# Moving a block of multiply-and-sums from the gate stretch into the attention stretch of a one-core hybrid layer

## The chip, the cores and the metric

The kernel runs on one core of a Trainium2 chip. The metric is device time in microseconds (us) of one execution. TensorE is called PE below (PEld is its weight load), VectorE DVE, ScalarE ACT, GpSimd POOL, and SP is the engine that issues most DMAs.

## What is computed

One layer for 128 context tokens and 512 latent tokens of width 1024. What matters here, cut from the reference:

```
mod = (silu(cond) @ w_ada + b_ada).reshape(N_MOD, D_MODEL)
shift1, scale1, gate1, shift2, scale2, gate2 = mod
h = rmsnorm(x, g_pre_mix) * (1 + scale1) + shift1
(na_q, na_k, na_v, m_q, m_k, m_v, m_o, m_i, m_f, cv_b, cv_c, cv_x, gate_pre) = split(h @ w_in)
s = concat(q @ k_neighbours + bias + column_mask, q @ k_ctx)      # 512 latent tokens, 8 heads x 64
p = softmax(s);  att = p_loc @ v_neighbours + p_ctx @ v_ctx
...                                                               # mLSTM branch hm, convolution branch hc
g = sigmoid(gate_pre + b_gate)
merged = g0 * (att @ w_br_na) + g1 * (hm @ w_br_m) + g2 * (hc @ w_br_cv)
x = x + gate1 * rmsnorm(merged @ w_out, g_post_mix)
h2 = rmsnorm(x, g_pre_ffn) * (1 + scale2) + shift2
x = x + gate2 * rmsnorm((silu(h2 @ w_ffn_gate) * (h2 @ w_ffn_up)) @ w_ffn_down, g_post_ffn)
```

The "late modulation" is the part of `mod` that nothing needs before the output projection: gate1, scale2 and shift2 (the code numbers them 2, 4 and 3). Each is 1024 columns, so eight blocks of 128 columns. There are 24 such blocks, each for two condition vectors (latent and context).

## The kernel before, in words

**Precision.** Large products are done in three passes on PE: each operand is split into a high part (`w_hi`, `h_hi`, rounded) and a rest (`w_lo`, `h_lo`), and `three` (lines 2106 to 2108) multiplies hi by hi, hi by lo and lo by hi. ACT makes the high part of a weight block (`split_hi`, line 1117), DVE the rest (`split_low`, line 1495).

**Weights.** All weights are stored as blocks of 128 x 1024 numbers (512 KB). SP loads them in one fixed order into a ring of four slots, `raw`. Block b goes to slot b % 4, and its load (line 854) waits until block b - 4 has been used up: for a weight, until its rest has been made (`lo_done`); for a block of the late modulation, until its sums are done (`ada_done`). `w_hi` and `w_lo` have four slots each too, and a slot is written again when PE has finished with the block in it.

**The plan.** `make_plan` writes out one list of steps, and every engine walks through the same list and takes from it what is its own, in order. So the place of a step in the list sets the order on each engine, and semaphores do the rest. `split` is the step that splits a weight block (or works on a block of the late modulation), `group` a product on PE with the drain of its PSUM bank.

**The stages around the change**, by time in the profile: the v projection ends at 57 us. Then come the projections q0, k0 (57 to 86 us), q1, k1, mq, mk and mv (86 to 242 us), each of groups of 24 matmuls of 320 columns. From 90 us on the attention is done beside them, in 18 units: 16 units of two heads and 16 query columns ("lat") and two of context ("ctx"). A unit's scores are made on PE in step `("na", 0, s)`, DVE adds bias and mask into `sx` (line 1822) and takes the row maximum (line 1825), ACT takes the exponential and the row sum (line 1365), DVE divides (lines 1838, 1841), PE transposes one unit later (line 2365), ACT copies (line 1375), and PE multiplies by the values two units later (line 2326). DVE then copies the result to `att` (line 1804).

**Bias and values.** Before the first unit two things must be there. POOL builds `bm`, bias plus mask, from `braw` in `bias(hp)` with six additions (line 1011); the first `braw` is loaded by SP (line 841). And the values must stand in another layout: POOL writes them to `vline` in DRAM with four DMAs (line 1036), and when all four have landed gathers them into `vtok` with eight DMAs of 256 KB (line 1042). On POOL these stand in this order: additions of `bias(0)`, load of the next `braw`, four writes, eight gathers. The first product with the values on PE waits for all eight.

**The late modulation before.** `ada_block` does a block: two `scalar_tensor_tensor` instructions on DVE (line 1508) multiply the 128 x 1024 block with a condition vector that stands in every partition (`condr`) and sum each row, one for each of the two vectors. The 24 blocks stand in the order of blocks between the gate and branch weights (467 to 611 us), with `ADA_PER_GATE` saying how many behind which. `condr` is loaded and passed through SiLU at 453 to 467 us. Two such blocks of the first modulation (`dot`, line 1763) are done in the same way at 39 to 50 us, with a copy of the condition vectors in `condr0`, whose place `naq` (the q of the attention) takes over afterwards.

Of the kernel before, what the change touches and what calls it, by code (L numbers as in the profile page):

```python
# [62 lines left out]
ADA_AHEAD, ADA_PER_GATE = 2, {2: (0, 0, 0, 0), 0: (1, 4, 4, 4), 1: (4, 4, 1, 0)}  # L63


def weight_units():
# [17 lines left out]
    late = [("ada", (m, j), KD, P) for m in (2, 4, 3) for j in range(KD)]  # L84
    for b in (2, 0, 1):
        if b == 0:
            u += [("mo", 0, KD, UW), ("mo", 1, KD, UW)] + [late.pop(0) for _ in range(ADA_AHEAD)]
        for i in range(4):
            u.append(("gate", (b, i), KD, UW))
            u.append(("br", (b, i), 4, UW))  # L90
            u += [late.pop(0) for _ in range(ADA_PER_GATE[b][i])]
# [6 lines left out]
    return u  # L98
# [21 lines left out]
BLOCKS = [(n, p) for n in range(len(UNITS)) for p in range(parts_of(n))]  # L120
# [13 lines left out]
UNIT_OF = {(k, w): n for n, (k, w, _, _) in enumerate(UNITS)}  # L134
NA_UNITS = ([("lat", hp, j) for hp in (0, 1) for j in range(NQB)] + [("ctx", 0, 0)]
# [35 lines left out]
def make_plan():  # L171
# [29 lines left out]
    def split_to(end):  # L201
        while ahead[0] < min(end, len(BLOCKS)):
            b = ahead[0]
            ahead[0] += 1
            plan.append(("split", b))
            if is_ada(b) and UNITS[BLOCKS[b][0]][1][1] == KD - 1:
                plan.append(("ada_fin", UNITS[BLOCKS[b][0]][1][0]))

    held = []
    side = []  # L210

    def unit(n):
        kind, which = UNITS[n][:2]
        for j, emit in enumerate(tiles(n)):
            later = 0
            if kind == "gate" and which[0] != 2:
                g0 = BLOCK_OF[n, 0]
                adas = ADA_PER_GATE[which[0]][which[1]]
                split_to(g0 + 3 + [adas // 2, (3 * adas + 3) // 4, adas, adas + (which != (1, 3))][j])
                if j % 2 == 0:  # L220
                    plan.append(("use", g0 + j // 2))
            elif kind == "br" and which[0] != 2 and which != (1, 3) and j == 0:
                split_to(BLOCK_OF[n, 0] + 3 + ADA_PER_GATE[which[0]][which[1]])
                plan.append(("use", BLOCK_OF[n, 0]))
            elif UNITS[n][:2] == ("br", (1, 3)):
# [27 lines left out]
            if side and j == 1 and UNITS[n][0] in ("q", "k", "mq", "mk"):  # L253
                plan.append(("half", len(groups)))
                plan.extend(side.pop(0))
# [62 lines left out]
    split_to(7)  # L318
    for t in range(TT):
        group("v", FIRST_ADA, t, bank=t if t < 4 else 7)  # L320
# [6 lines left out]
    while UNITS[n][0] != "out":  # L327
        kind, which = UNITS[n][0], UNITS[n][1]
        if kind != "ada":
            if kind == "mif":  # L330
# [4 lines left out]
                plan.append(("na_end",))  # L335
            elif kind == "mv":
                for t in range(TT):
                    for j in range(4):
                        if t == 0:
                            split_to(BLOCK_OF[n, 3] + 1)  # L340
                            plan.append(("use", BLOCK_OF[n, j]))
                        if side and (j % 2 == 0 or t == TT - 1):
                            plan.extend(side.pop(0))
# [178 lines left out]

def holder(b):

    b -= BLOCKS_HELD
    while b >= 0 and is_ada(b):
        b -= BLOCKS_HELD
    return b
# [49 lines left out]
def program(nc, a, out, vline, gline, xline):  # L578

    ctx = ExitStack()  # L580
    with ctx:
# [11 lines left out]
        def chain(start, *items):  # L593

            got = []
            for name, shape, dt in items:
# [65 lines left out]
        prod = [at("prod0", [P, D], MG - 2 * 1056 - 2048),  # L662
                at("prod1", [P, D], MG - 2 * 1056 - 3 * 2048 - 128 - 640 - 2560)]
# [21 lines left out]
        def sems(names):  # L685
# [16 lines left out]
        condr_in, condr_rd, ada_done, gcol_rd, gl_tr, gl_row, gl_out, g1_in, g2_in = sems(  # L702
            "condr_in condr_rd ada_done gcol_rd gl_tr gl_row gl_out g1_in g2_in")
# [17 lines left out]
        na_sc, na_add, na_max, na_exp, na_prob, na_tr, na_pt, na_pv, na_out = sems(  # L721
            "na_sc na_add na_max na_exp na_prob na_tr na_pt na_pv na_out")
# [90 lines left out]
        def held(buf, b):  # L813
# [3 lines left out]
            return buf[:, b % BLOCKS_HELD, :]  # L817
# [27 lines left out]
        def _(sp):  # L845
# [37 lines left out]
            for step in PLAN:  # L883
                if step[0] == "split":
# [3 lines left out]
                    elif step[1] + BLOCKS_HELD < len(BLOCKS):  # L888
                        load(step[1] + BLOCKS_HELD)
# [1656 lines left out]
```

## Time and profile before

| what | value |
|---|---|
| runs | 1143.97 us median of 3 (1143.1 to 1144.38) |
| profiled execution, first to last instruction | 1140.5 us, of its own time the part that the profile spans |
| PE busy | 1123.8 us (99%) |
| DVE busy | 725.8 us (64%) |
| ACT busy | 478.3 us (42%) |
| POOL busy | 70.8 us (6%) |
| chain that ended last | PE 93%, DVE 4% |
| granted PE clock | 0.998 over the span |

The median of the runs is 3.5 us above the span of the profiled execution; that is what lies before its first and behind its last instruction. The kernel uses one core, so there is no second die to compare with. PE's ends are modelled in the profile, so its busy time also counts overlaps: what tells of lost time is the start of one matmul against the start of the next.

### The profile page before, as it was taken

What the parts mean: (1) busy time and instruction counts of PE and PEld (TensorE: products, weight loads), DVE (VectorE), ACT (ScalarE), POOL (GpSimd) and SP (SyncE); (2) the same over time, 40 slices, a digit from 0 to 9 for tenths busy, and PEclk for the clock granted to TensorE, in tenths of its full rate; (3) what the DMA queues carried; (4) which work ended last, traced back from release to release, by engine and by line L of the source; (5) the groups of instructions that cost most, each with busy time, mean ns of one, the idle gap of its engine ahead of it and who ended that gap; (6) DMA issues with size and microseconds to landing.
All of it is one profiled execution on the core that took longest, in us unless ns stands there. A gap on an engine that the chain in (4) does not pass through costs nothing.

```text
span 1140.5 us, 18499 instructions
## 1 busy us (share of the span) xinstructions
PE 1123.8 (99%) x7324; PEld 1057.9 (93%) x7324; DVE 725.8 (64%) x1297; ACT 478.3 (42%) x881; POOL 70.8 (6%) x123
## 2 busy tenths in 40 slices
PE   6999999999999999999999999999999999999997
PEld 5799999889999999999999988999999999988886
DVE  5724444459575665687894546899897777633444
ACT  5624444344333344322222337645555455533431
POOL 2051111000000000400000002000000000000002
PEclk9999999999999999999999999999999999999999
DMA  9665221132522112346654235143332232315112
GB/s 374 241 208 120 74 75 38 38 111 80 70 58 72 57 57 73 128 125 189 192 184 128 74 130 165 58 162 122 124 111 75 75 140 83 111 64 195 56 37 93
DMA packets 40151, 130.22 MB, mean 114 GB/s; under 512 B 8737, under 2 KB 10305, under 8 KB 38529
## 3 DMA queue, kind: packets, MB, share of 16 engines
q1 hardware_dynamic: 36592, 121.41, 33.0%
q0 software_dynamic: 3472, 7.62, 2.4%
q8 instruction: 59, 0.97, 0.4%
q14 instruction: 28, 0.22, 0.1%
HBM read 121.64 MB, written 7.36 MB: 113 GB/s over the span
## 4 chain that ended last, share of the span: by engine, by line
PE 93%; DVE 4%; ACT 1%; issue 1%; DMA 0%; POOL 0%; POOLq 0%; SPq 0%; ACTq 0%; DVEq 0%
PE ps L2106 28%; PE ps L2108 28%; PE ps L2107 28%; PE ps L2326 1%; PE ps L2365 1%; PE ps L2349 1%; PE ps L2412 1%; PE ps L2414 1%; PE ps L2293 1%; PE ps L2416 1%; PE ps L2153 0%; PE ps L2400 0%; DMA xt<-in_x_sample 0%; DVE w_lo L1495 0%; PE ps L2398 0%
## 5 line engine op out<-in xcount | busy, mean ns | idle before, releaser
L2108 PE MATMUL ps<-h_hi,w_lo 128*128 128x320 f32 x1184 | 365.8, 309 | 0.0
L2106 PE MATMUL ps<-h_hi,w_hi 128*128 128x320 f32 x1024 | 322.5, 315 | 0.2 <-DVE w_hi L1620 0.2
L2107 PE MATMUL ps<-h_lo,w_hi 128*128 128x320 f32 x1024 | 316.3, 309 | 0.0
L2108 PEld LDWEIGHTS ps<-h_hi,w_lo 128*128 128x128 f32 x1184 | 222.3, 188 | 0.0
L1495 DVE TENSOR_TENSOR w_lo<-raw,w_hi 128x1024 fp32r<-128x1024 f32 x109 | 132.8, 1228 | 107.8 <-ACT w_hi L1117 107.3
L2106 PEld LDWEIGHTS ps<-h_hi,w_hi 128*128 128x128 f32 x1024 | 192.4, 188 | 2.4 <-DVE w_hi L1620 0.5
L2107 PEld LDWEIGHTS ps<-h_lo,w_hi 128*128 128x128 f32 x1024 | 192.5, 188 | 0.1
L2106 PE MATMUL ps<-w_hi,h_hi 128*128 128x512 f32 x378 | 149.3, 395 | 0.0
L2108 PE MATMUL ps<-w_hi,h_lo 128*128 128x512 f32 x378 | 147.3, 390 | 0.0
L2107 PE MATMUL ps<-w_lo,h_hi 128*128 128x512 f32 x378 | 147.1, 389 | 0.0
L1117 ACT ACTIVATE w_hi<-raw 128x1024 fp32r<-128x1024 f32 x109 | 113.2, 1052 | 32.8 <-PE ps L2108 32.2
L2106 PEld LDWEIGHTS ps<-w_hi,h_hi 128*128 128x128 f32 x378 | 71.0, 188 | 16.3 <-issue 1.6
L2108 PEld LDWEIGHTS ps<-w_hi,h_lo 128*128 128x128 f32 x378 | 70.9, 188 | 15.1
L2107 PEld LDWEIGHTS ps<-w_lo,h_hi 128*128 128x128 f32 x378 | 71.0, 188 | 14.1
L1208 ACT ACTIVATE gt<-ps,half_bg 128x320 f32<-128x320 f32 x48 | 25.4, 528 | 137.5 <-PE ps L2108 137.5
L2106 PE MATMUL ps<-h_hi,w_lo 128*128 128x320 f32 x240 | 74.4, 310 | 0.8 <-ACT snap L1255 0.8
L2106 PE MATMUL ps<-tt_hi,w_hi 128*128 128x320 f32 x240 | 74.2, 309 | 0.0
L2107 PE MATMUL ps<-tt_lo,w_hi 128*128 128x320 f32 x240 | 74.2, 309 | 0.0
L2108 PE MATMUL ps<-tt_hi,w_hi 128*128 128x320 f32 x240 | 74.2, 309 | 0.0
L2107 PE MATMUL ps<-h_lo,w_lo 128*128 128x320 f32 x240 | 74.2, 309 | 0.0
L1541 DVE TENSOR_TENSOR h_lo<-ff,h_hi 128x1280 fp32r<-128x1280 f32 (+1 forms) x22 | 30.5, 1428 | 64.4 <-ACT h_hi L1145 64.4
L1508 DVE SCALAR_TENSOR_TENSOR prod<-raw,condr 128x1024 f32<-128x1024 f32 x48 | 57.0, 1225 | 14.5 <-ACT condr L1329 12.9
(284 smaller groups left out, 1826.9 us busy)
## 6 DMA issues: line engine op xcount, KB each, us to landing
raw<-in_w_blocks SPq DMA_DIRECT2D x182, 512.0 KB, 3.8
ada<-in_w_first SPq DMA_DIRECT2D x8, 1024.0 KB, 19.9
xline<-x SPq DMA_DIRECT2D x5, 512.0 KB, 5.2
x<-xline SPq DMA_DIRECT2D x5, 512.0 KB, 8.0
xt<-in_x_sample SPq DMA_DIRECT2D x4, 512.0 KB, 5.1
condr<-in_cond_rows POOLq DMA_DIRECT2D x2, 1024.0 KB, 7.9
vtok<-vline POOLq DMA_DIRECT2D x8, 256.0 KB, 10.7
g<-gline SPq DMA_DIRECT2D x2, 1024.0 KB, 6.7
```

What stands on the lines that cost most here:

```text
L1117: ins = nc.scalar.activation(held(w_hi, b), raw[:, s, :], ACT.Copy)
L1208: nc.scalar.activation(gt[:, f, half(h)], bank, ACT.Tanh, scale=0.5, bias=half_bg[:, t:t + 1]).then_inc(act_drain, 1)
L1495: nc.vector.tensor_tensor(held(w_lo, b), raw[:, s, :], held(w_hi, b).bitcast(F32), ALU.subtract).then_inc(lo_done, 1)
L1508: ins = nc.vector.scalar_tensor_tensor(prod[c][:, :], raw[:, b % BLOCKS_HELD, :], 1.0, condr[:, c, :], ALU.mult, ALU.mult, accum_out=to)
L1541: nc.vector.tensor_tensor(h_lo[:, o2 + k:o2 + k + n, :], ff[:, k0 + k:k0 + k + n, :], h_hi[:, o2 + k:o2 + k + n, :].bitcast(F32), ALU.subt ...
L2106: nc.tensor.matmul(dst, wh, xh, start=first, stop=False, skip_group_check=resumed)
L2107: nc.tensor.matmul(dst, wh, xl, start=False, stop=False, skip_group_check=resumed)
L2108: return nc.tensor.matmul(dst, wl, xh, start=False, stop=last, skip_group_check=resumed)
L2293: ins = nc.tensor.transpose(turned_x(t, hh)[:, kk, :], xt[:, t, tok(4 * hh + kk)], ident)
L2326: ins = nc.tensor.matmul(dst[:, NKEY:512], src, pt[:, n % 2, i, c * P:(c + 1) * P], start=(c == 0), stop=(c == 2))
L2349: nc.tensor.matmul(A[i][:, 0:256], q, kk, start=True, stop=True)
L2365: ins = nc.tensor.transpose(A[2 + i][:, c * P:(c + 1) * P], sx[:, n % 2, i, c * P:(c + 1) * P], ident)
```

## The change

Three things are changed.

1. The 24 blocks of the late modulation move in the order of blocks (`EARLY_RING`) from the gates to between the blocks of k0 to mv, and on DVE to 58 to 210 us in the times of before: eight blocks before the first attention unit, then one to each of the first 15 units, and one more in mk0. A block is done in halves (`ada_half`): the product with the first vector right behind the row maximum of a unit, the second behind its division. The second half writes its products over the block itself. The weights' own splits keep their order, but stand one to two steps later or earlier. `w_hi` and `w_lo` slots are now counted by weights alone (`w_slot`).
2. The condition vectors are now `conda`, a copy of `condr0` by one SBUF to SBUF DMA of 1 MB on SP. It is issued between the load of block 10 and the load of the first `braw`. ACT's first write of `naq` waits for it, and so does the first half. `condr` is still loaded at 453 us, for a later use (line 1683).
3. Bias addition and row maximum, one addition of 768 and one reduction of 768 for a unit, become two `tensor_tensor_reduce` of 384, one for a head, that add, change the sign, and give the minimum. ACT's exponential takes the sign back by its scale. PE and POOL wait for `na_max` where they waited for `na_add`.

The order of PE's instructions is the same before and after, line by line.

```
+LATE_ADAS = [(m, j) for m in (2, 4, 3) for j in range(8)]
+EARLY_RING = ("v.0 v.1 v.2 v.3 q0.0 q0.1 k0.0 + k0.1 + + q1.0 + + q1.1 + + k1.0 "
+              "+ + k1.1 + mq0.0 + mq0.1 + mq1.0 + + mq1.1 + mk0.0 + mk0.1 + mk1.0 + + + mk1.1 + mv.0 "
+              "+ mv.1 + mv.2 +").split()
...
     split_to(7)
+    plan.append(("conda",))
...
+                elif step[0] == "ada_rest":
+                    load(step[1] + BLOCKS_HELD)
+                elif step[0] == "conda":
+                    sp.wait_ge(condr0_rd, 1)
+                    sp.wait_ge(dot_done, 2 * len(DOT_CHUNKS))
+                    sp.wait_ge(gemm_done, gid("ada_row", ("first", DOT_CHUNKS[0] - 1)) + 1)
+                    sp.dma_start(conda[:, :, :], condr0[:, :, :]).then_inc(conda_in, 16)
...
                     act.wait_ge(gemm_done, g + 1)
+                    if (which, f, h) == (0, 0, 0):
+                        act.wait_ge(conda_in, 16)
...
+            def ada_half(b, c):
...
+                s = b % BLOCKS_HELD
+                if c == 0:
+                    dve.wait_ge(raw_in[s], 16 * (b // BLOCKS_HELD + 1))
+                    if adas_done(b) == 1:
+                        dve.wait_ge(conda_in, 16)
+                    else:
+                        dve.wait_ge(ada_done, adas_done(b) - 1)
+                to = gcol[:, 0, c, i:i + 1] if m == 2 else mod[:, 2 if m == 4 else 3, i, c:c + 1]
+                spent = conda[:, 0, :] if adas_done(b) == len(LATE_ADAS) else prod[:, :]
+                ins = nc.vector.scalar_tensor_tensor(raw[:, s, :] if c else spent, raw[:, s, :], 1.0, conda[:, c, :],
+                                                     ALU.mult, ALU.mult, accum_out=to)
+                if c:
+                    ins.then_inc(ada_done, 1)
...
-                                nc.vector.tensor_tensor(sx[:, b], ps[:, 4:6, 0:NKEY], bm[:, BTYPE[j]],
-                                                        ALU.add).then_inc(na_add, 1)
-                                dve.wait_ge(na_add, s + 1)
-                                nc.vector.tensor_reduce(small[:, 16:18], sx[:, b], X, ALU.max, negate=True).then_inc(na_max, 1)
+                                for i in range(2):
+                                    ins = nc.vector.tensor_tensor_reduce(
+                                        sx[:, b, i, :], A[i][:, 0:NKEY], bm[:, BTYPE[j], i, :], -1.0, 3e38,
+                                        ALU.add, ALU.min, small[:, 16 + i:17 + i])
+                                ins.then_inc(na_max, 1)
```

**SP, from the last loads of the start on.** Before:

```order
17 L854 DMA raw<-in_w_blocks 128x1024 x7
18 L841 DMA braw<-in_rpb 128x1024
19 L854 DMA raw<-in_w_blocks 128x1024 x21
20 L907 DMA out_k<-sx 128x8x64
21 L910 DMA out_v<-vtok 128x8x64
```

Of the change:

```order
17 L919 DMA raw<-in_w_blocks 128x1024 x7
18 L961 DMA conda<-condr_84 128x2048
19 L906 DMA braw<-in_rpb 128x1024
20 L919 DMA raw<-in_w_blocks 128x1024 x45
21 L979 DMA out_k<-sx 128x8x64
```

The copy now stands ahead of the first `braw`, and 24 more blocks of 512 KB are loaded up to the end of the attention.

**DVE, from the end of the v projection to the first attention unit.** Before:

```order
58 L1570 TENSOR_SCALAR lf<-ps,gbias 36x320
59 L1495 TENSOR_TENSOR w_lo<-raw,w_hi 128x1024 x5
60 L1822 TENSOR_TENSOR sx<-ps,bm 128x768
61 L1825 TENSOR_REDUCE small<-sx 128x2
62 L1838 RECIPROCAL small<-small 128x2
```

Of the change:

```order
58 L1653 TENSOR_SCALAR lf<-ps,gbias 36x320
59 L1590 SCALAR_TENSOR_TENSOR prod,gcol<-raw,conda 128x1024
60 L1590 SCALAR_TENSOR_TENSOR raw,gcol<-raw,conda 128x1024
...
76 L1575 TENSOR_TENSOR w_lo<-raw,w_hi 128x1024
77 L1590 SCALAR_TENSOR_TENSOR prod,gcol<-raw,conda 128x1024
78 L1590 SCALAR_TENSOR_TENSOR raw,gcol<-raw,conda 128x1024
79 L1603 TENSOR_TENSOR gcol<-gcol,cols 128x8x2
80 L1606 TENSOR_TENSOR gcol<-gcol,cols 128x8x2
81 L1910 ISA sx,small<-ps,bm 128x384
82 L1910 ISA small 128x1
83 L1910 ISA sx,small<-ps,bm 128x384
84 L1910 ISA small 128x1
85 L1590 SCALAR_TENSOR_TENSOR prod,mod<-raw,conda 128x1024
86 L1925 RECIPROCAL small<-small 128x2
87 L1928 TENSOR_SCALAR sx<-sx,small 128x384 x2
```

Between `lf` and the first row maximum DVE now does eight blocks of the modulation (rows 59 to 78, four weight rests between them), where five weight rests stood. In each of the first 15 units one half comes before the division and one after it. The two ISA rows of a head are the fused instruction and the reading of its minimum.

## Rows read from the trace of the kernel before

**Rows 1.** The page: engines, the late modulation's instruction (busy us, mean ns, idle before).

```profile
PE 1123.8 (99%) x7324; PEld 1057.9 (93%) x7324; DVE 725.8 (64%) x1297; ACT 478.3 (42%) x881; POOL 70.8 (6%) x123
...
L1508 DVE SCALAR_TENSOR_TENSOR prod<-raw,condr 128x1024 f32<-128x1024 f32 x48 | 57.0, 1225 | 14.5 <-ACT condr L1329 12.9
```

**Rows 2.** PE's longest wait by what released it: total us, times, longest.

```profile
PE ps L2293 <- DVE xt L1734: 8.2, 1, 8.2
```

**Rows 3.** Stretches: busy us of each engine (instructions), clock, DMA share, GB/s.

```profile
90.00:240.00 150.00, 150.00 (x1118) 135.36 (x1115) 69.44 (x124) 63.16 (x143) 14.13 (x20) 1.00 0.21 60
...
500.00:640.00 140.00, 140.00 (x959) 139.93 (x957) 101.44 (x172) 35.33 (x51) 0.00 (x0) 1.00 0.51 158
```

**Rows 4.** Timeline of DVE in one attention unit: start, us, what, idle before it.

```profile
112.52 0.96 DVE L1822 TENSOR_TENSOR sx<-ps,bm 128x768 f32<-128x768 f32 x1 [0.51 <-PE ps L2350]
113.51 0.95 DVE L1825 TENSOR_REDUCE small<-sx 128x2 f32<-128x768 f32 x1
117.25 1.23 DVE L1495 TENSOR_TENSOR w_lo<-raw,w_hi 128x1024 fp32r<-128x1024 f32 x1 [2.79 <-ACT w_hi L1117]
118.39 0.16 DVE L1838 RECIPROCAL small<-small 128x2 f32<-128x2 f32 x1
118.59 0.75 DVE L1841 TENSOR_SCALAR sx<-sx,small 128x384 f32<-128x384 f32 x2
119.51 0.29 DVE L1804 COPY att<-ps 128x128 f32<-128x128 f32 x1 [0.17 <-PE ps L2326]
```

**Rows 5.** Timeline of DVE at the early multiply-and-sums, two in a row.

```profile
45.97 1.22 DVE L1763 SCALAR_TENSOR_TENSOR dot<-ada,condr 128x1024 f32<-128x1024 f32 x1
47.12 0.08 DVE L1763 DVE_READ_ACCUMULATOR dot<-ada,condr 128x1 f32 x1
```

**Rows 6.** Timeline of SP, 53 to 100 us.

```profile
54.42 3.06 SPq L854 DMA_DIRECT2D raw<-in_w_blocks  x3
57.52 0.43 SPq L841 DMA_DIRECT2D braw<-in_rpb  x1
```

**Rows 7.** Timeline of POOL, 55 to 110 us.

```profile
64.26 5.19 POOL L1011 TENSOR_TENSOR bm<-braw,cst 128x256 f32<-128x256 f32 x6 [4.76 <-DMA braw<-in_rpb]
...
70.33 2.15 POOL L1036 DMA_DIRECT2D vline<-vst  x4
78.21 5.45 POOL L1042 DMA_DIRECT2D vtok<-vline  x8 [5.73 <-DMA vline<-vst]
```

**Rows 8.** The gathers, 77 to 101 us: durations, first and last start, landing.

```profile
L1042 POOL DMA_DIRECT2D vtok<-vline x8: 679/679/734, 78.2 to 83.0; - x8
...
DMA to landing us min/median/max: 2.7/10.7/16.3
```

**Rows 9.** Timeline of PE where the first values and the second scores are used.

```profile
94.18 0.71 PE L2349 MATMUL ps<-nak,naq 64*128 64x256 f32 x4
...
102.93 0.88 PE L2326 MATMUL ps<-pt,vtok 128*64 128x128 f32 x12
```

**Rows 10.** DMAs: condr (1 MB, issued at 453 us); raw (512 KB each, 100 to 240 us).

```profile
L1062 POOL DMA_DIRECT2D condr<-in_cond_rows x1: 540/540/540, 453.4 to 453.4; - x1
...
DMA to landing us min/median/max: 5.0/5.0/5.0
...
DMA to landing us min/median/max: 3.4/3.6/4.3
```

**Rows 11.** POOL's additions (min/median/max ns) and the DVE instruction beside the slow one.

```profile
L1011 POOL TENSOR_TENSOR bm<-braw,cst x6: 731/732/1707, 64.3 to 68.7; 128x256 f32<-128x256 f32 x6
...
66.55 1.62 DVE L1495 TENSOR_TENSOR w_lo<-raw,w_hi 128x1024 fp32r<-128x1024 f32 x1 [5.62 <-ACT w_hi L1117]
```

**Rows 12.** DMA, 78 to 100 us: all, and raw loads' median to landing.

```profile
DMA packets 2619, 3.77 MB, mean 172 GB/s; under 512 B 1707, under 2 KB 1707, under 8 KB 2617
...
raw<-in_w_blocks SPq DMA_DIRECT2D x3, 512.0 KB, 10.6
```

**Rows 13.** POOL's pass over mo: min/median/max ns, eight instructions, four beside a busy DVE.

```profile
L1068 POOL TENSOR_SCALAR mo<-mo x8: 461/612/1451, 453.9 to 483.2; 128x320 f32<-128x320 f32 x8
```

More of the change, by code:

```diff
@@ L83, in weight_units @@
         u += [("cc", p, KD, UW), ("cx", p, KD, UW), ("cb", p, KD, UW)]
-    late = [("ada", (m, j), KD, P) for m in (2, 4, 3) for j in range(KD)]
     for b in (2, 0, 1):
         if b == 0:
-            u += [("mo", 0, KD, UW), ("mo", 1, KD, UW)] + [late.pop(0) for _ in range(ADA_AHEAD)]
+            u += [("mo", 0, KD, UW), ("mo", 1, KD, UW)]
         for i in range(4):
@@ L97, in weight_units @@
             u.append(("down", (c, i), DOWN_TILES[i], 512))
-    return u
+    return u + [("ada", which, KD, P) for which in LATE_ADAS]
 UNITS = weight_units()
@@ L117, in parts_of, with ring_order @@
     return 0 if kind == "mif" else kc * w // 1024
-BLOCKS = [(n, p) for n in range(len(UNITS)) for p in range(parts_of(n))]
+def ring_order():
+    first_ada = len(UNITS) - len(LATE_ADAS)
+    rest = [(n, p) for n in range(first_ada) for p in range(parts_of(n))]
+    late = [(n, 0) for n in range(first_ada, len(UNITS))]
+    order = []
+    for x in EARLY_RING:
+        order.append((late if x == "+" else rest).pop(0))
+        n, p = order[-1]
+        kind, which = UNITS[n][:2]
+        assert x == "+" or x == f"{kind}{'' if kind in ('v', 'mv') else which}.{p}", x
+    return order + rest
+BLOCKS = ring_order()
 BLOCK_OF = {np_: b for b, np_ in enumerate(BLOCKS)}
@@ L215, in unit @@
             later = 0
[L216 to L225, printed above, removed]
+            if UNITS[n][:2] == ("br", (1, 3)):
                 if j == 0:
@@ L520, in adas_done, with w_slot @@
     return sum(1 for i in range(b + 1) if is_ada(i))
+def w_slot(b):
+    return (hi_ready(b) - 1) % BLOCKS_HELD
 def holder(b):
[L525 to L528, printed above, removed]
+    held = [x for x in range(b) if not is_ada(x) and w_slot(x) == w_slot(b)]
+    return held[-1] if held else -1
 def origin(b):
@@ L887, in _ @@
                         load_wide(*divmod(step[1] - W0, 2))
[L888 removed]
+                    elif step[1] + BLOCKS_HELD < len(BLOCKS) and not is_ada(step[1]):
                         load(step[1] + BLOCKS_HELD)
+                elif step[0] == "ada_rest":
[5 more added lines that the diff above has]
+                    sp.dma_start(conda[:, :, :], condr0[:, :, :]).then_inc(conda_in, 16)
                 elif step[0] == "wu" and step[2] == 0:
```

110 lines of the change are left out of this document (75 added, 35 removed).

## The prediction

> **What bounds the kernel now.** I read the page first. PE is busy for 1123.8 of 1140.5 us, DVE for 725.8, and the moved instructions are 57.0 us of DVE [rows 1]. The next question is whether PE ever waits for what they keep DVE from. PE's waits say no: the largest, 8.2 us, is for the first x at the start [rows 2], and no wait on DVE in the gates is listed. The table of stretches says the same in another way. In the gates (500 to 640 us) DVE is busy for 101.4 of 140 us, and PE starts 959 matmuls, one every 146 ns. In the attention (90 to 240) DVE is busy for 69.4 of 150 us [rows 3]. So the place that is relieved costs nothing today, and the place that is loaded has room on average. What is left to ask is where in the loaded place something ends late. The timelines of SP, POOL, DVE and PE from 53 to 105 us answer that.
>
> **The gates.** 48 products and their readings leave DVE. PE keeps its order and its 146 ns. Worth to the end: 0.0 us, at most the 0.3 us by which 959 starts at 146.0 ns exceed their usual distance in this stretch, if all of it were due to DVE, which nothing shows.
>
> **One attention unit on DVE.** Before, from the rows of one unit [rows 4]: addition 0.96, maximum 0.95, weight rest 1.23, reciprocal 0.16, division 0.75, copy 0.29, in all 4.34 us in a unit of some 7.8 us (24 matmuls and the unit's own). The change takes out 0.96 + 0.95 = 1.91 and puts in two fused instructions of 384. No row shows one. From below, they are one pass over 768 elements, 0.96. From above, each costs as much as a pass over 768, so 1.91 together. I take 1.1: an addition of 768 in two pieces, with the fixed part of an instruction once more. It adds two products of 1.15 us start to start, their reading included [rows 5], so 2.3. A unit is then 4.34 - 1.91 + 1.1 + 2.3 = 5.8 us, and 6.6 at the upper bound. Both fit into 7.8. Over 90 to 240 us DVE gets 16 blocks x 2.3 = 37 us more and 16 x 0.8 = 13 less: 93 of 150. What PE needs of a unit, the divided exponentials, it uses one unit later. So the first half of a block ahead of the division, which stands where DVE waits for ACT anyway, costs PE nothing; if that cover is gone, it is 1.15 us later in a slack of about four. Cost: 0.
>
> That price for a product goes by the trace, 1.22 us for 1024 elements of two fp32 tiles in SBUF with the sum taken [rows 5], the same as the plain weight rest of 1.23 [rows 4]. The Trainium skill (Vector Engine (DVE) Microarchitecture Reference, section 7) says that this shape of instruction has half its throughput with two such sources. By that rule, as an estimate, a block would take 4.5 us, a unit 4.34 - 1.91 + 1.1 + 4.5 = 8.0 us, and DVE would bind the attention by 0.2 us in each of 15 units, 3 us in all. The trace has the very instruction at full rate, so the rule gets neither a term nor a chance.
>
> **Before the first unit.** Eight blocks and four weight rests stand there: 8 x 2.3 + 4 x 1.2 = 23.2 us. They can begin when `conda` has landed. SP issues it at about 57.5 us, where it issued `braw` before [rows 6]. 1 MB landed in 5.0 us and 512 KB in 3.6, in 3.4 at the least [rows 10], so 512 KB more costs about 1.5 us, and 1 MB about 3.0. `braw` was there at 64.26, when POOL began [rows 7]; `conda` goes ahead of it and lands about when `braw` did, less its own 512 KB: 65.7 us. DVE is then full to about 89 us, and scores of the first unit are ready at 90.6. It just fits. ACT's first write of `naq`, at 61.6 us, waits for the copy, about 4 us; the bank it empties is wanted four groups (14 us) later. Cost: 0.
>
> **The chain that does not fit.** It is on SP, POOL and the DMA engines. PE's first product with the values starts at 102.93 us [rows 9]. The last of the eight gathers was issued at 83.0 and took 16.3 us, so it landed at 99.3 [rows 8]. Slack: 3.6 us. The chain back from it is: gathers after the four writes landed (78.21), writes after the six additions of `bias(0)`, additions after `braw` (64.26) [rows 7]. Three things lengthen it.
> 1. `braw` behind the 1 MB copy: +3.0 us. Bounds: 1.5 (the copy moves at twice the rate, since it leaves DRAM alone) and 5.0 (nothing overlaps).
> 2. The six additions now run beside a DVE that is never idle. Five of them took 0.73 us, and the one that met a DVE instruction took 1.71, while that instruction took 1.62 instead of 1.23 [rows 11]: POOL and DVE waited for each other. POOL's pass over `mo` shows the same, 0.46 us alone and 0.61 to 1.45 beside a busy DVE [rows 13]. Bounds: 0, if no addition meets one, and 6 x 0.98 = 5.9. I take 0.6 each, near the middle of what the `mo` passes lost: +3.6 us. DVE loses 0.4 each, 2.4 us, which moves the first maximum to about 92.5; the second scores want it at 94.2 [rows 9].
> 3. While the gathers run, the DMA engines are full and move only 172 GB/s; three raw loads fell in this window, and their median was 10.6 us to landing instead of 3.6 [rows 8, 10, 12]. Each more load of 512 KB in it costs 3.0 us of that rate. Bounds: 0 (they share it only with idle gaps) and three loads, 9. The first halves want a block every 3 to 4 us here, but a ring of four slots at 10 us each gives few. I take one: +3.0 us.
>
> Sum: 3.0 + 3.6 + 3.0 - 3.6 = **6.0 us** that PE waits at 103 us. PE is the bound everywhere after, so nothing gives it back, and the wait gives DVE and the ring time to catch up. The span goes from 1140.5 to 1146.5, and with the 3.5 us around it the time from 1143.97 to **1150.0 us**.
>
> **The end of the attention.** The last block is done by about 206 us. ACT waits for it in two drains, of mk1 and of the second mv at 221 us; both come later than the sums. The weight rests of mv.3 and of the convolution keep their places. Cost: 0. The extra instructions on SP are loads only.
>
> **Rivals.**
> - *It hides* (no change, 1144 to 1146). Only the copy's 3.0 us come true, the additions slip between DVE's instructions, and the loads fill gaps of the DMA engines. It decides at 3.6 us: below that sum, PE never waits. For it speaks that POOL's instructions met DVE's with small loss in two of the four `mo` passes (0.61); against it, that two of them lost far more and that the DMA engines have no gaps there.
> - *DVE starves for blocks* (about 1155). A half waits for its block, and the maximum of a unit stands behind it in DVE's queue. A block issued at 82 us with 11 us to land is there at 93; its two products and the first maximum end at 93 + 2.3 + 1.1 = 96.4, and PE wants that at 94.2: 2.2 us. The next turn of the ring costs as much again, about 3 us, and the gathers' 6.0 come on top: 11 us. It decides where a block that the first unit needs is issued after the gathers begin. For it: raw loads of 10.6 us. Against: DVE takes eight blocks before, and most are issued before 79 us.
> - *The gates get faster* (1141 or less). DVE's reads would have to slow PE's in the gates. For it speaks only that DVE is fuller there; against it, PE starts a matmul every 146 ns there too.
> - That the change does not do what it says is excluded: the order of instructions shows the 24 blocks in their new places, and PE's order unchanged.
>
> **Chances.** 0.2% of this kernel is 2.3 us, about what a measurement can tell from no change. Gather chain late by 3 to 9 us: 0.45. Starved DVE: 0.19. Hidden, or late by under 2.3: 0.31. Faster: 0.05. So faster 0.05, same 0.31, slower 0.64. The range goes from 1143.5, which takes in the hidden case, to 1158.0, the starved case with three more loads in the gathers' window. It leaves out the faster case and the ends of the others, some 2 in 10.
>
> **What would show it.** In the changed profile: `conda` landing at 65 to 66 us and `braw` 3 us later than before; POOL's six additions longer than 0.73 us each; the first of the gathers at 84 to 86 us instead of 78.2; PE idle before the first product with the values (line 2326 of before), released by the DMA of `vtok`, and nearly all of the difference there. A fused instruction of about 0.55 us; DVE at about 60% in the attention and 40 to 45% in the gates, with PE at 146 ns a start in both. I am wrong if the gathers land before 103 us and PE still loses time, or if PE waits for `small` (the maximum) instead, which is the starved case, or if PE's starts in the gates come closer together.

## The result, and the profile after

The changed kernel takes 1164.03 us (median of 4 runs, 1162.14 to 1165.01), the kernel before 1143.53 in the same comparison (4 runs, 1142.95 to 1144.38). The ratio is 1.0175, 95% interval 1.0162 to 1.0187: 20.5 us slower. I had forecast 1150.0, in a range to 1158.0. The place and the mechanism were the ones named, the size was not. In the chain that ends with the gathers, the gathers' window was to grow by 3.0 us and grew by 8.3, the writes were to cost nothing more and cost 4.4, and the two other terms were somewhat small; and PE lost time in two places to which the sum gave nothing.

PE's waits of the changed kernel (engine, what waits, what released it: us in total, times, longest), which answer to [rows 2]:

```profile
PE ps L2413 <- DMA vtok<-vline: 13.3, 1, 13.3
PE ps L2380 <- DVE xt L1821: 8.8, 1, 8.8
PE ps L2436 <- ACT nak L1256: 2.6, 1, 2.6
PE ps L2461 <- DVE mnat L2013: 1.3, 1, 1.3
```

Three of the four are new. The order of PE's instructions is the same in both programs, so the k-th matmul of one trace can be set against the k-th of the other; where the distance between the two grows, time is lost, and nowhere else:

| where (us after) | step by which PE falls behind | what |
|---|---|---|
| up to 50 | +0.8 | the start; in the runs below it is 0.4 to 2.2, whatever the kernel |
| 93.13 | +2.7 | first scores (L2436) wait for ACT's drain of k |
| 94 to 98 | +1.5 | lower PE clock behind that wait |
| 121.36 | +13.4 | first values (L2413) wait for the gathers |
| 122 to 126 | +1.7 | lower PE clock behind that wait |
| 289.07 | +1.2 | first product of the mLSTM (L2461) waits for `mnat` |
| 290 to the end | -0.3 | |

The sum is 21.0 us, the difference of the spans (1161.5 - 1140.5). From 126 us on PE keeps its pace but for the 1.2. The stretches say so too; these answer to [rows 3], with two short ones behind PE's two long waits (columns as there):

```profile
90.00:240.00 150.00, 134.09 (x1001) 123.05 (x1000) 101.13 (x224) 59.56 (x129) 29.18 (x29) 0.94 0.49 142
500.00:640.00 140.00, 140.00 (x962) 139.90 (x962) 58.36 (x97) 35.64 (x52) 3.58 (x4) 1.00 0.26 83
```

```profile
94.00:98.00 4.00, 4.00 (x19) 4.00 (x18) 3.89 (x12) 0.85 (x2) 3.22 (x6) 0.57 0.83 203
...
121.00:126.00 5.00, 4.64 (x28) 3.95 (x29) 1.73 (x6) 0.36 (x1) 0.32 (x1) 0.58 0.00 0
```

In the gates PE still starts a matmul every 146 ns (140 us / 962), with DVE at 42% instead of 72%. In the attention it starts 1001 in place of 1118. The granted clock of 0.57 and 0.58 is a mean over a stretch that goes from the lower level (1.2 GHz) back to the full one.

Where the 13.4 us come from is read off the chain of waits, cut to 58 to 121 us (start, us, what):

```profile
58.46 0.54 SPq L961
58.99 0.04 issue
59.04 9.42 DMA braw<-in_rpb
68.45 0.07 issue
68.53 10.02 POOL bm L1083 x6
78.55 0.29 issue
78.84 0.58 POOL braw L906
79.42 1.61 POOL vline L1107 x3
81.03 10.44 DMA vline<-vst
91.47 0.28 issue
91.75 4.76 POOL vtok L1113 x7
96.51 24.61 DMA vtok<-vline
121.12 0.24 issue
121.36 1.55 PE ps L2413 x12
```

Set beside [rows 7, 8], link by link:

| link | before | after | longer by | forecast |
|---|---|---|---|---|
| `braw` there (1.0 of it is issued later by the start) | 64.19 | 68.45 | 4.3 | 3.0 |
| six additions | 5.2 | 10.0 | 4.8 | 3.6 |
| last write, issue to landing | 6.0 | 10.4 | 4.4 | none |
| last gather, issue to landing | 16.3 | 24.6 | 8.3 | 3.0 |
| sum: last gather there | 99.27 | 121.12 | 21.8 | 9.6 |

The last link is there 21.85 us later. PE itself comes 5.07 us later by then, and of the slack of 3.66 us 0.24 are left, so 3.42 are used up: 21.85 - 5.07 - 3.42 = 13.36.

The second place is ACT. Its timeline in the changed kernel before the first scores:

```profile
83.51 0.44 ACT L1256 ACTIVATE nak<-ps 128x320 f32<-128x320 f32 x1 [0.43 <-PE ps L2195]
91.70 1.06 ACT L1190 ACTIVATE w_hi<-raw 128x1024 fp32r<-128x1024 f32 x1 [7.75 <-DMA raw<-in_w_blocks]
92.66 0.42 ACT L1256 ACTIVATE nak<-ps 128x320 f32<-128x320 f32 x1
```

The last drain of k (L1256), which the first scores need, stands in ACT's queue behind the high part of a weight block, and that block's load landed at 91.67, 7.2 us after its issue, beside the four writes. Two things meet here. Blocks of the modulation stand ahead of this weight in the ring, two for each weight, so it is asked for late. And the change also moved ACT's high parts: in the kernel before they stand behind the drain of the same group, now they stand one drain earlier. The same place in the kernel before:

```profile
86.19 0.44 ACT L1179 ACTIVATE nak<-ps 128x320 f32<-128x320 f32 x1 [3.08 <-PE ps L2108]
86.53 1.05 ACT L1117 ACTIVATE w_hi<-raw 128x1024 fp32r<-128x1024 f32 x1
```

### The profile page after: what moved, and what is told of

Its sections match the earlier page's. It is cut to its first block, busy times and chain, and to the rows that moved or that the text cites. A ratio compares the mean times of both kernels' runs of the same rounds, so it can differ in the third digit from the quotient of the medians.

```text
span 1161.5 us, 18521 instructions
## 1 busy us (share of the span) xinstructions
PE 1126.5 (97%) x7324; PEld 1059.7 (91%) x7324; DVE 720.8 (62%) x1329; ACT 479.2 (41%) x881; POOL 83.8 (7%) x123
## 4 chain that ended last, share of the span: by engine, by line
PE 85%; DMA 5%; DVE 5%; ACT 2%; POOL 2%; issue 1%; SPq 1%; POOLq 0%; ACTq 0%; DVEq 0%
PE ps L2193 26%; PE ps L2194 26%; PE ps L2195 26%; DMA vtok<-vline 2%; DMA ada<-in_w_first 1%; PE ps L2413 1%; PE ps L2452 1%; DMA vline<-vst 1%; POOL bm L1083 1%; PE ps L2436 1%; DMA braw<-in_rpb 1%; PE ps L2499 1%; PE ps L2501 1%; PE ps L2503 1%; DVE w_lo L1575 1%
## 5 line engine op out<-in xcount | busy, mean ns | idle before, releaser
L1287 ACT ACTIVATE gt<-ps,half_bg 128x320 f32<-128x320 f32 x48 | 25.3, 528 | 113.8 <-PE ps L2195 113.8
L1334 ACT ACTIVATE snap<-ps 128x320 f32<-128x320 f32 x80 | 35.0, 437 | 63.3 <-PE ps L2195 63.3
## 6 DMA issues: line engine op xcount, KB each, us to landing
ada<-in_w_first SPq DMA_DIRECT2D x8, 1024.0 KB, 20.2
```

The source lines that it names most:

```text
L1287: nc.scalar.activation(gt[:, f, half(h)], bank, ACT.Tanh, scale=0.5, bias=half_bg[:, t:t + 1]).then_inc(act_drain, 1)
L1334: nc.scalar.activation(snap[:, i, :], wbank(w, 1 if i == 2 else 0), ACT.Copy).then_inc(fsnap, 1)
```

## The experiments

All are compared with the kernel before, run on the same chip at the same time. "Behind" is PE's distance to the kernel before, read as above.

**Which of the loads and the products.**

e1: the loads are cut to 64 of 1024 columns, the products stay.

```
-                sp.dma_start(raw[:, b % BLOCKS_HELD, :], source(b))...
+                w = 64 if is_ada(b) else 1024
+                sp.dma_start(raw[:, b % BLOCKS_HELD, 0:w], source(b)[:, 0:w])...
```

> The changed kernel, but each of the 24 blocks of the late modulation is loaded in its first 64 of 1024 columns only (32 KB in place of 512 KB); the products still run over all 1024 columns, over what stands there, so gate1, scale2 and shift2 come out wrong. Theory A (the chain copy, braw, six additions, four writes, eight gathers is late, and three things share it: the 1 MB copy, GpSimd's additions slowed by VectorE, and above all the raw loads that share the DMA engines with writes and gathers): VectorE's work and GpSimd's additions stay (10 us), the writes land in about 6 us instead of 10.4, the last gather 16 us after its issue instead of 24.6; so the gathers are there at about 109 us, PE waits 4 to 5 us in place of 13.3, the 2.6 us at the first scores go, and the time is 1149 to 1152. Rival B (VectorE's own work in the attention makes PE late, the loads do not matter): 1161 or more.

e2: the products are cut to 64 of 1024 columns, the loads stay.

```
-                ins = nc.vector.scalar_tensor_tensor(raw[:, s, :] if c else spent, raw[:, s, :], 1.0, conda[:, c, :],
+                ins = nc.vector.scalar_tensor_tensor(raw[:, s, 0:64] if c else spent, raw[:, s, 0:64], 1.0, conda[:, c, 0:64],
```

> The changed kernel, but each of the 48 products of the late modulation runs over 64 of 1024 columns; loads and copy stay whole. gate1, scale2 and shift2 come out wrong. Theory A: GpSimd's six additions take about 5 us again instead of 10, and braw, writes and gathers still share the DMA engines with the copy and with the loads, which now come as early as the ring allows, so more of them lie before the writes: gathers there at 108 to 116 us, time 1150 to 1158. Rival B (VectorE's work): everything back, 1144 to 1146. Both experiments together: theory A has e1 win back more than e2.

e1 took 1151.09 us (ratio 1.0071, 1.0057 to 1.0084), e2 1157.93 (1.0119, 1.0101 to 1.0136). PE's waits for the gathers, the additions, and the gathers' landing (min, median, max), of e1:

```profile
PE ps L2414 <- DMA vtok<-vline: 4.8, 1, 4.8
```

```profile
67.06 9.27 POOL L1084 TENSOR_TENSOR bm<-braw,cst 128x256 f32<-128x256 f32 x6 [5.75 <-DMA braw<-in_rpb]
```

```profile
DMA to landing us min/median/max: 2.7/13.4/18.0
```

and of e2:

```profile
PE ps L2413 <- DMA vtok<-vline: 12.5, 1, 12.5
```

```profile
70.06 6.19 POOL L1083 TENSOR_TENSOR bm<-braw,cst 128x256 f32<-128x256 f32 x6 [8.44 <-DMA braw<-in_rpb]
```

```profile
DMA to landing us min/median/max: 5.6/12.2/22.6
```

So each does what theory A said: without the products the additions take 6.2 us instead of 10.0, without the bytes the last gather takes 18.0 instead of 24.6 and the last write 7.5 instead of 10.4, and no wait at the first scores is left in either. (The profiled execution of e1, 1154.62 us, is the slowest of its four: behind its wait of 1.2 us at the mLSTM it lost another 3.0 us at a lower PE clock.) The bytes are the larger part, and rival B (VectorE's work alone) falls: with nearly all of that work gone, e2 still waits 12.5 us. The winnings do not sit cleanly in one link. In e2 the blocks are used up faster, so more raw loads lie beside the writes: the last write took 11.1 us.

**The other two parts of the change.**

e3: the kernel before with the fused instruction (the two lines of the diff above, and the scale of the exponential). e4: e3, and the copy to `conda` ahead of `braw` on SP, which nothing reads.

> The kernel before with one part of the change alone: bias addition and row maximum as one instruction per head, the sign taken back in the exponential. Theory A: VectorE takes 1.1 us for it instead of 1.9 and nothing waits for that, so within 0.2% of before, 1142 to 1146. Rival C (the fused instruction or the later release of the score banks to PE costs the time): 1150 or more, with PE waiting for small or at the scores.

> The kernel before with the fused instruction of e3 and the 1 MB copy of the condition vectors ahead of the first braw, which nothing reads; no block of the modulation is moved. Theory A: braw lands 3 to 4.5 us later than before, the last gather about as much later, against a slack of 3.6 us: PE waits 0 to 1 us, time 1143 to 1146. Rival D (the copy alone sets the chain back by far more than its own bytes): PE waits 3 us or more before the first product with the values, 1147 or more.

e3 took 1143.74 us (1.0004, 0.9995 to 1.0012), e4 1143.84 (1.0000, 0.9991 to 1.0009). Both are the kernel before, as far as a measurement tells. The fused instruction in e3 (ns min/median/max) and PE's wait in e4:

```profile
L1824 DVE CUSTOM_DVE_ANT_0 sx<-ps,bm x32: 545/553/560, 92.1 to 220.0; 128x384 f32<-128x384 f32 x32
```

```profile
PE ps L2337 <- DMA vtok<-vline: 0.3, 1, 0.3
```

In e4 `braw` landed at 70.16 us, in e3 at 65.29: 4.9 us for the copy, a little above what I expected, and about 0.6 of it by the start. The last gather landed 6.0 us later than in e3. The slack just holds it. So the copy alone costs nothing, but it has used up the slack before the first moved block is loaded. Taken over e4, the products add 7.3 us (e1 - e4), the loads 14.1 (e2 - e4), both together 20.2: nearly additive (the 1.2 us at the mLSTM are in all three).

**The order of the chain.**

e5: the first `braw` ahead of the copy on SP.

```
                     sp.wait_ge(gemm_done, gid("ada_row", ("first", DOT_CHUNKS[0] - 1)) + 1)
+                    load_bias(sp, br0_in, 0)
                     sp.dma_start(conda[:, :, :], condr0[:, :, :]).then_inc(conda_in, 16)
...
-                elif step[0] == "kc":
...
-                    load_bias(sp, br0_in, 0)
```

> The changed kernel with the first braw issued ahead of the 1 MB copy on SP. Theory A: braw lands 2 to 4 us earlier than in the changed kernel, the additions, writes and gathers follow, PE's wait falls from 13.3 to 9.5 to 11.5 us, time 1160 to 1162. That the order of the two is what costs the time (rival D): under 1150.

e6: the four writes ahead of the additions. e7: writes and gathers ahead of them.

```
                     pool.dma_start(vtok[:, 9, :], a["cache_v"]).then_inc(vc_in, 16)
+                    for t in range(CH):
+                        pool.wait_ge(act_drain, drains("A", gid("v", 0, t)))
+                        pool.dma_start(vline[tok(t), :], vst[:, t, :]).then_inc(v_out, 16)
                     bias(0)
...
-                    for t in range(CH):
-                        pool.wait_ge(act_drain, drains("A", gid("v", 0, t)))
-                        pool.dma_start(vline[tok(t), :], vst[:, t, :]).then_inc(v_out, 16)
```

> The changed kernel with GpSimd's four writes of the values to vline moved ahead of the six additions; the gathers stay behind them. The writes then wait neither for braw nor for the additions and land while the additions run. Theory A (the chain is copy, braw, additions, writes, gathers, each link's length added up): gathers issued at 79 to 82 us instead of 91.8, the last there at 103 to 110 us, PE waits 0 to 4 us before the first product with the values instead of 13.3, time 1150 to 1155. Rival B (VectorE): no change, 1162 or more.

> The changed kernel with writes and gathers both ahead of the six additions on GpSimd. Theory A: gathers issued from about 70 us, there before 100 us, no wait before the first product with the values; the additions end at 84 to 88 us, just in time for the first maximum. What stays is the slow raw loads, which now lie beside the gathers before 95 us: PE waits 2 to 5 us for a weight block or the first scores, and the 1.2 us at the mLSTM. Time 1147 to 1152. Rival B: 1162 or more.

| run | time, ratio (interval) | last gather there | PE waits for gathers | PE waits at first scores |
|---|---|---|---|---|
| e5 | 1154.78, 1.0103 (1.0086 to 1.0120) | 111.7 | 0 | 8.1 |
| e6 | 1155.93, 1.0121 (1.0087 to 1.0155) | 113.8 | 0 | 7.2 |
| e7 | 1156.96, 1.0116 (1.0100 to 1.0131) | 102.3 | 0 | 9.4 |

I was wrong on e5, which won 9 us where I had given it 2 to 4. With `braw` first, POOL begins while DVE still waits for `conda`, so of the additions at most one meets a DVE instruction (e5's POOL; the changed kernel has 10.0 there):

```profile
66.77 5.19 POOL L1081 TENSOR_TENSOR bm<-braw,cst 128x256 f32<-128x256 f32 x6 [6.03 <-DMA braw<-in_rpb]
```

I was wrong on e7 as well, in the other direction, and e6 ended 0.9 us above its range: it has no wait for the gathers, but 7.2 us at the first scores that I had not expected. In all three the wait for the gathers is gone, and a wait of the same family has taken its place: ACT's last drain of k behind a raw load. Whoever brings the gathers forward lays them beside the loads which the first scores hang on.

e8: the weight rest of mv in its old place.

```
-                            split_to(BLOCK_OF[n, j] + BLOCKS_HELD + 1)
+                            split_to(BLOCK_OF[n, j] + BLOCKS_HELD + 1 + (j < 3))
```

> The changed kernel with one split in mv put back where it stood (three high parts ahead of the last drain of mv, not two): the changed kernel's count of blocks takes the late modulation's into account and so splits one block later. In the changed kernel VectorE has one weight rest of 1.2 us more to do before the key output and the mLSTM's statistics, and PE starts the mLSTM's first product 1.2 us later beside its own delay. Expected: this 1.2 us goes, nothing else, time 1162 to 1163.5 against 1164.0 (a difference of 1.2 us is near what the runs can tell; the profile's wait of PE for mnat, 1.3 us, tells it). If the wait comes from elsewhere, it stays.

The time was 1161.92 us (1.0158, 1.0130 to 1.0187), just below what I expected, which alone doesn't tell it from the changed kernel. PE's wait does:

```profile
PE ps L2461 <- DVE mnat L2013: 0.2, 1, 0.2
```

**How many blocks ahead of the first unit.**

e9: three in place of eight, none in unit 0, seven more between later units; and e8. e10: e9 with e5 and e6. e12: e10 with the eight blocks again.

```
+ADA_FIRST = {("q", 0, 1), ("q", 0, 2), ("q", 0, 3)}
+ADA_EXTRA = {("k", 1, 2), ("mk", 0, 0), ("mk", 0, 3), ("mk", 1, 2), ("mq", 0, 0), ("mq", 0, 3), ("mq", 1, 2)}
...
-            if not side and (kind, which, j) != ("q", 0, 0) or (kind, which, j) == ("q", 1, 0):
+            if (kind, which, j) in ADA_FIRST:
...
-            if (kind, which, j) == ("mk", 0, 0):
+            if (kind, which, j) in ADA_EXTRA:
```

> The changed kernel with three blocks of the late modulation ahead of the first attention unit in place of eight, none in unit 0, and seven more as a whole block between two units later (in k1, mq and mk); all 24 stay in the projections. The rest of mv stands where it stood, as in e8. Theory A: two to five blocks fewer are loaded while writes and gathers are under way, and VectorE leaves GpSimd's additions alone for half of their time. braw is 3.4 to 4.3 us later than before, the additions 1 to 3, the writes 0 to 1, the gathers 0 to 3: the last lands at 104 to 109 us, PE waits 0 to 4 us there, none at the first scores, time 1144 to 1149. If VectorE's work as such is the trouble (rival B), the later blocks bring it back in units that carry 8.1 us of work in 7.8: PE waits for small or w_lo between 130 and 220 us, 1150 or more.

> e9 with the two repairs of the chain on top: the first braw ahead of the copy (e5) and the writes to vline ahead of the six additions (e6). Theory A: the gathers are issued at 73 to 77 us, 1 to 5 us ahead of those of before, and land by 98 us; no wait at the gathers and none at the first scores, time 1142 to 1146, that is no difference from before that can be told (0.2%). If 2 us or more are left, they stand at the first scores (raw loads beside the gathers), and the time is 1146 to 1149.

> e10 with the eight blocks of the changed kernel ahead of the first unit again (the changed kernel, with the first braw ahead of the copy, the writes ahead of the additions, and the weight rest of mv in its old place): it tells whether the order alone repairs the chain or the number of blocks counts too. Theory A (what counts is how many bytes are asked of the DMA engines while the gathers run): the gathers are there in time for the values, but the raw loads behind which ACT's k drain stands take 11 to 14 us each, PE waits 6 to 10 us at the first scores as in e5, e6 and e7, time 1150 to 1155. If the order alone decides (rival D): 1143 to 1146.

| run | time, ratio (interval) | last gather there | PE waits for gathers | PE waits at first scores |
|---|---|---|---|---|
| e9 | 1154.15, 1.0097 (1.0083 to 1.0110) | 111.4 | 7.8 | 0 |
| e10 | 1143.17, 0.9997 (0.9988 to 1.0006) | 104.4 | 0 | 0 |
| e12 | 1160.45, 1.0153 (1.0138 to 1.0168) | 102.8 | 0 | 10.6 |

e9 came out 5 us above the range that I expected, and so did e12. The gathers are back at 16.3 us to landing, but the additions are not: three blocks (3 x 2.3) and the rests between them still keep DVE busy for the 10 us in which POOL adds.

```profile
68.64 10.15 POOL L1086 TENSOR_TENSOR bm<-braw,cst 128x256 f32<-128x256 f32 x6 [8.30 <-DMA braw<-in_rpb]
```

e10 is as fast as the kernel before, with all 24 blocks in the projections. Its gathers, issued at 72.8 us, still take 26.9 to land, since nine raw loads are issued in that time, but they start early enough (the last is there 0.8 us before PE comes to it, at 105.2), and the weights of k are asked for early enough. POOL's timeline:

```profile
61.72 2.14 POOL L1103 DMA_DIRECT2D vline<-vst  x4
66.91 4.21 POOL L1084 TENSOR_TENSOR bm<-braw,cst 128x256 f32<-128x256 f32 x6 [3.04 <-DMA braw<-in_rpb]
...
72.75 5.44 POOL L1114 DMA_DIRECT2D vtok<-vline  x8 [0.77 <-DMA vline<-vst]
```

The later units carry the seven blocks without a wait: DVE is busy for 110.9 of 150 us between 90 and 240, PE for all 150. e12 settles that it is not the order of SP's and POOL's instructions alone. ACT's timeline of e12:

```profile
83.50 1.06 ACT L1188 ACTIVATE w_hi<-raw 128x1024 fp32r<-128x1024 f32 x1 [10.50 <-DMA raw<-in_w_blocks]
...
91.67 1.06 ACT L1188 ACTIVATE w_hi<-raw 128x1024 fp32r<-128x1024 f32 x1 [6.39 <-DMA raw<-in_w_blocks]
...
101.50 1.06 ACT L1188 ACTIVATE w_hi<-raw 128x1024 fp32r<-128x1024 f32 x1 [8.12 <-DMA raw<-in_w_blocks]
102.46 0.42 ACT L1254 ACTIVATE nak<-ps 128x320 f32<-128x320 f32 x1
```

Three weight blocks in a row are waited for, with two blocks of the modulation ahead of each in a ring of four, and each load taking 9 to 13 us. Theory A had put e12's loss down to the bytes asked for while the gathers run. That does not tell e10 from e12: ten raw loads are issued in that window in e12 and nine in e10, and the last gather takes 25.4 and 26.9 us. What e10 has over e12 is that fewer blocks stand ahead of k's weights and of the first row maximum. That left open whether the number of blocks does it or ACT's order, in which the drain stands behind the high part. Two more runs put ACT's order back; in both only ACT's rows change. e13 is the changed kernel with it, e14 is e12 with it.

```
-            if j % 2 and len(coming) > (j == 1):
-                split_block(*coming.pop(0))
             emit()
+            if j % 2 and len(coming) > (j == 1):
+                split_block(*coming.pop(0))
```

> The changed kernel with the high parts of the weights on ACT behind the drain of the same group, where they stand in the kernel before; in the changed kernel they stand one drain earlier, ahead of the last drain of k. Only ACT's order differs. Theory A (the wait of 2.6 us at the first scores is this order meeting a slow raw load, and the gathers are a chain of their own): the wait at the first scores goes, the wait for the gathers grows by what PE is earlier, 3 to 4.5 us, to 16 to 18 us, time within 2 us of the changed kernel, 1162 to 1166. If more of the loss hangs on ACT's order (theory E): under 1160.

> e12 (eight blocks ahead, braw first, writes first, rest of mv in its old place) with ACT's high parts behind the drains as well. Its gathers are there in time, so it tells whether e12's 10.6 us at the first scores come from ACT's order alone. Theory E (the order alone): the first scores start at 91 to 93 us, no other wait takes over, 1143 to 1146. Theory A (the number of blocks counts: eight blocks and four rests must be loaded and done ahead of the first row maximum, the last of them landed at 101.5 us in e12): the scores are on time, but VectorE reaches the first maximum at about 103 us, or the next weights are late, and PE waits 5 to 10 us in all for small, pt or w_lo, 1149 to 1156.

e13 took 1164.09 us (1.0186, 1.0170 to 1.0202), the changed kernel's time. The wait at the first scores is gone and a wait for VectorE's first row maximum stands in its place, ahead of the second scores. So PE is late for the gathers by nearly as much as in the changed kernel (3.8 us against 4.2, the start taken off), and that wait does not grow to the 16 to 18 us that I expected:

```profile
PE ps L2413 <- DMA vtok<-vline: 13.0, 1, 13.0
...
PE ps L2436 <- DVE small L1910: 2.1, 1, 2.1
```

e14 took 1155.61 us (1.0112, 1.0095 to 1.0129), with no wait for the gathers. At the first scores 1.5 us are left: two drains of k stand behind the high part before them, whose block landed only at 89.9 us. PE's longest wait after the start, and DVE's timeline up to the first row maximum:

```profile
PE ps L2434 <- DVE small L1908: 9.0, 1, 9.0
```

```profile
94.78 1.23 DVE L1588 SCALAR_TENSOR_TENSOR prod<-raw,conda 128x1024 f32<-128x1024 f32 x1 [2.61 <-DMA raw<-in_w_blocks]
...
100.11 1.22 DVE L1573 TENSOR_TENSOR w_lo<-raw,w_hi 128x1024 fp32r<-128x1024 f32 x1 [0.15 <-ACT w_hi L1188]
...
104.11 0.56 DVE L1908 CUSTOM_DVE_ANT_0 sx<-ps,bm 128x384 f32<-128x384 f32 x1
```

So ACT's order costs part (e14 against e12: 4.8 us) and is not the whole cause. Eight blocks and four weights must be loaded and done ahead of the first maximum; with the gathers beside them the last is done at 104 us, where the forecast had the first maximum at 92.5. That is the rival of a starved DVE, which in the changed kernel stood hidden behind ACT's wait. Which of e5, e6 and e8 are needed in e10 was not tried one by one.

**The gates.** e11: the kernel before with its 48 products over 64 columns, in their old places.

```
-                    ins = nc.vector.scalar_tensor_tensor(prod[c][:, :], raw[:, b % BLOCKS_HELD, :], 1.0, condr[:, c, :],
+                    ins = nc.vector.scalar_tensor_tensor(prod[c][:, 0:64], raw[:, b % BLOCKS_HELD, 0:64], 1.0, condr[:, c, 0:64],
```

> The kernel before with its 48 late products over 64 of 1024 columns, in their old places in the gates (gate1, scale2 and shift2 come out wrong): the gates are relieved of nearly all their VectorE work there, and nothing is added elsewhere. Theory A (the gates are worth nothing): 1142 to 1146, and PE still starts one matmul every 146 ns between 500 and 640 us. The rival that the gates get faster: under 1141.

It took 1143.50 us (1.0000, 0.9991 to 1.0008). The gates, with DVE at 61.0 of 140 us:

```profile
500.00:640.00 140.00, 140.00 (x959) 139.93 (x958) 61.03 (x176) 35.25 (x51) 0.00 (x0) 1.00 0.46 158
```

959 starts, as before. Relieving DVE there is worth nothing.

## Why the prediction was right and wrong

The step that failed is the sum of the gather chain, 3.0 + 3.6 + 3.0 - 3.6 = 6.0 us. Its term 3, the gathers' window, measured 8.3 in place of 3.0, and the four writes, which had no term, measured 4.4. Beside it, "Before the first unit, cost 0" failed by 2.7 us and the clock behind that wait. Step by step:

- *The gates, worth 0*: right (e11; 962 starts in the changed kernel).
- *The attention unit, 5.8 us of DVE, cost 0*: right in the cost, and in the size but for what POOL adds. DVE is busy for 101.1 of 150 us, where the forecast had 93. From the changed kernel, with the fused pair at 0.96 us start to start (I had 1.1) and a product at 1.23:

```profile
132.68 0.56 DVE L1910 CUSTOM_DVE_ANT_0 sx<-ps,bm 128x384 f32<-128x384 f32 x1 [0.23 <-PE ps L2437]
...
133.64 1.22 DVE L1590 SCALAR_TENSOR_TENSOR prod<-raw,conda 128x1024 f32<-128x1024 f32 x1
...
135.30 1.23 DVE L1928 TENSOR_SCALAR sx<-sx,small 128x384 f32<-128x384 f32 x2
136.56 1.23 DVE L1590 SCALAR_TENSOR_TENSOR raw<-raw,conda 128x1024 f32<-128x1024 f32 x1
```

  This unit comes to 6.3: the division takes 1.23 instead of 0.75 where an addition of POOL's next `bias` meets it. The product's full rate holds, 1.22 us for 1024 elements from two fp32 tiles in SBUF; the rule of the Trainium skill on this shape (Vector Engine (DVE) Microarchitecture Reference, section 7), by which, as an estimate, a block would take 4.5 us, is contradicted by the 48 products here too.
- *Before the first unit, cost 0*: wrong, by 2.7 us and the 1.5 of clock. I counted DVE's work against the time ("it just fits") and let the blocks be there when it wanted them. The rival "DVE starves for blocks" had the cause right. What it missed is that ACT, with the high parts one drain earlier, is held up by the same loads first; with that taken away (e13) DVE's first maximum is 2.1 us late, as the rival had it (2.2), and the time is the same.
- *Term 1, braw +3.0*: right within its bounds (3.3 without the later start; 4.9 in e4 against e3, start included).
- *Term 2, six additions +3.6*: too small, 4.8, within the bounds. I took a loss of 0.6 for each from passes that DVE met now and then; beside a DVE that never rests every one of the six takes 1.6 to 1.73 us, the full price. e1 (9.3 us) and e2 (6.2) bear it out.
- *Missing term: the writes.* Four DMAs of 256 KB stand in the chain between additions and gathers, and I let them cost what they had cost. They took 4.4 us more: five raw loads were issued beside them in place of one, and with the bytes of the moved blocks cut (e1) the last write took 7.5 us instead of 10.4.
- *Term 3, the gathers' window +3.0*: wrong, 8.3 us, near its upper bound of 9. I took one more load, at 3.0 us. Seven were issued in the window in place of three, and two were under way at its start in place of one. So the count was far too low and the price too high: four more loads for 8.3 us are 2.1 each. The price rested on DMA engines that are full in the kernel before; from 78 to 100 us they are busy for 85% there. The argument "a ring of four gives few at 10 us each" looked at the loads' duration and not at how many slots came free at once: eight blocks and their rests are used up one after the other, and each frees a slot.
- *Slack 3.6*: right, and spent by the copy alone (e4).
- *The end of the attention, cost 0*: wrong by 1.2 us. The rests of mv did not keep their places: a count of blocks ahead that was right before now counts blocks of the modulation too (e8).
- *The clock*: not in the sum. 3.2 us, behind the two waits.

The loss by these steps, with what was measured: gathers 13.4, first scores 2.7, clock 3.2, mLSTM 1.2, start 0.8, less 0.3 at the end.

## What to carry to other kernels

An engine with room on average is not what a moved block of work must fit into: count what it asks of every shared thing in the stretch where it lands (bytes for the DMA engines, GpSimd's instructions beside VectorE's, slots of the load ring), and follow each chain of DMAs there link by link, writes too. When a ring is shared, take the wait away and look who is next: here the loads held up first the gathers, then ACT's k drain, then VectorE's first maximum. Where the chain can't be made shorter, start its DMAs earlier, and put fewer of the moved blocks ahead of what needs the ring next. Neither alone was enough here (e5, e6, e9, e12 and e14 each lost 11 to 17 us), both together lost nothing (e10), although its gathers still took 26.9 us.

## What was not expected of the hardware

- GpSimd's addition of 256 elements per partition takes 0.73 us alone (six in a row 4.21 in e10) and 1.60 to 1.73 in each of the six beside a busy VectorE. VectorE pays as well: single products of 1.75 in place of 1.22.
- While the gathers run, the DMA engines are busy for 91% and move 216 GB/s; in the 12.5 us before, busy for 95%, they moved 330 GB/s (the changed kernel; columns as in [rows 3]):

```profile
79.00:91.50 12.50, 11.51 (x79) 11.25 (x77) 10.16 (x17) 1.83 (x3) 2.57 (x5) 1.00 0.95 330
91.50:121.00 29.50, 14.94 (x94) 14.17 (x94) 16.42 (x33) 9.64 (x20) 7.88 (x10) 0.78 0.91 216
```

- After PE had been idle for 2.6 us, the granted clock went to the lower level from 94.6 to 97.8 us, and matmuls started every 267 ns instead of every 147. That cost 1.5 us, nearly as much as after the wait of 13.3 us (1.7). A wait of 1.2 us at the mLSTM in e1 was followed by a lower clock that cost 3.0 us, one of 1.3 us at the same place in the changed kernel by none; why is not shown. Two of PE's rows behind the wait of 2.6 us:

```profile
95.41 0.47 PE L2193 MATMUL ps<-h_hi,w_hi 128*128 128x320 f32 x1
95.68 0.47 PE L2194 MATMUL ps<-h_lo,w_hi 128*128 128x320 f32 x1
```
